# Two PEER blocks on one core: row pieces of the modulation on VectorE, other fillers, eight places for the value tiles

## The reference, cut to what matters

```python
mod = einsum('bd,de->be', c, w_mod) + b_mod
sh1, sc1, gt1, sh2, sc2, gt2 = split(mod, 6)
...
def peer_ffn(h, w_query, sub_keys, expert_u, expert_v):
    q = (h @ w_query)                          # 8 heads, two halves
    sc = einsum('bshpc,hpnc->bshpn', q, sub_keys)
    s1, i1 = top_k(sc[..., 0, :], 16); s2, i2 = top_k(sc[..., 1, :], 16)
    top_s, sel = top_k(s1[..., :, None] + s2[..., None, :], 16)   # over the 256 pairs
    idx = 128 * i1[sel] + i2[sel]; gates = softmax(top_s)
    a = gelu(einsum('cd,chkd->chk', x, expert_u[idx])) * gates
    return einsum('chk,chkd->cd', a, expert_v[idx])
```

## Time and profile before

| | us |
|---|---|
| median of 3 runs (lowest to highest) | 1972.68 (1967.51 to 1976.87) |
| the profiled execution | 1963.73 |
| its span | 1961.9 |
| PE, DVE, ACT, POOL busy | 1893.8, 1622.2, 1085.0, 568.2 |

### The profile page before, as it was taken

How to read it: one execution, slowest core, us unless ns; L and a number is a source line. 1 busy time by engine, 2 the same in 40 slices (tenths; PEclk the granted TensorE clock), 3 DMA queues, 4 the chain that set the end, 5 groups by cost and what they waited for, 6 DMA issues and landing times.

```text
span 1961.9 us, 36055 instructions
## 1 busy us (share of the span) xinstructions
PE 1893.8 (97%) x13546; PEld 1841.5 (94%) x13546; DVE 1622.2 (83%) x3384; ACT 1085.0 (55%) x2128; POOL 568.2 (29%) x498
## 2 busy tenths in 40 slices
PE   7999889999999999999999999999999999999997
PEld 5998889999999999999999988999999999999997
DVE  3777768889899989889777775588888998898997
ACT  3345555644566665555556554465445665555554
POOL 0000221444533234445200000034354332444351
PEclk8999999999999999999999999999999999999999
DMA  8764667678699899999856672566887898999995
GB/s 345 271 236 162 254 210 228 226 271 310 242 319 317 303 358 360 347 347 356 321 204 203 252 252 79 169 213 218 285 290 267 316 319 298 343 356 345 361 337 194
DMA packets 143469, 543.85 MB, mean 277 GB/s; under 512 B 15744, under 2 KB 16128, under 8 KB 138432
## 3 DMA queue, kind: packets, MB, share of 16 engines
q1 hardware_dynamic: 99312, 363.38, 52.7%
q0 software_dynamic: 40608, 160.06, 22.5%
q10 hardware_dynamic: 3376, 18.11, 2.5%
HBM read 539.78 MB, written 1.05 MB: 276 GB/s over the span
## 4 chain that ended last, share of the span: by engine, by line
PE 66%; DVE 13%; DMA 9%; issue 6%; ACT 5%; POOL 1%; SPq 0%; ACTq 0%; DVEq 0%; POOLq 0%
PE PB L1021 16%; PE PB L997 14%; PE PB L1022 7%; DVE WL L1813 5%; DMA RING<-in_v 5%; PE PB L994 4%; PE PB L959 4%; PE PB L586 4%; PE PB L587 4%; PE PB L588 4%; DMA RING<-in_u 3%; ACT WH L1324 2%; PE PB L992 2%; PE PB L908 2%; DVE AR L1838 1%
## 5 line engine op out<-in xcount | busy, mean ns | idle before, releaser
L1813 DVE TENSOR_TENSOR WL<-RING,WH 128x1024 fp32r<-128x1024 f32 x517 | 640.0, 1240 | 194.1 <-ACT WH L1324 190.1
L1324 ACT ACTIVATE WH<-RING 128x1024 fp32r<-128x1024 f32 x517 | 545.4, 1056 | 446.2 <-DMA RING<-in_v 161.2
L1021 PE MATMUL PB<-HX,WH 128*128 128x384 f32 x2048 | 587.7, 360 | 8.0 <-DVE WL L1813 7.4
L1022 PE MATMUL PB<-HX,WL 128*128 128x192 f32 x2048 | 512.7, 250 | 0.0
L1021 PEld LDWEIGHTS PB<-HX,WH 128*128 128x128 f32 x2048 | 384.5, 188 | 12.3 <-issue 11.7
L1022 PEld LDWEIGHTS PB<-HX,WL 128*128 128x128 f32 x2048 | 391.1, 191 | 0.0
L997 PE MATMUL PB<-AR,RING 128*128 128x192 f32 x2144 | 372.1, 326 | 0.0
L997 PEld LDWEIGHTS PB<-AR,RING 128*128 128x128 f32 x2144 | 348.1, 190 | 0.0
L2571 POOL DMA_INDIRECT AR<-in_v,SPX x128 | 244.6, 1911 | 320.8 <-DVE AR L2284 268.1
L994 PE MATMUL PB<-HX,WH 128*128 128x384 f32 x854 | 254.1, 361 | 0.0
L992 PE MATMUL PB<-HX,WL 128*128 128x192 f32 x976 | 227.8, 254 | 0.0
(11 more groups left out here) (277 smaller groups left out, 2891.2 us busy)
## 6 DMA issues: line engine op xcount, KB each, us to landing
RING<-in_u SPq DMA_DIRECT2D x256, 512.0 KB
RING<-in_v SPq DMA_DIRECT2D x256, 512.0 KB
RING<-in_win SPq DMA_DIRECT2D x90, 512.0 KB
AR<-in_wr POOLq DMA_DIRECT2D x24, 1024.0 KB, 5.4
RING<-in_wq SPq DMA_DIRECT2D x32, 512.0 KB
AR<-in_wr ACTq DMA_DIRECT2D x12, 1024.0 KB, 6.6
AR<-in_wm SPq DMA_DIRECT2D x8, 1024.0 KB, 16.4
RING<-in_wout SPq DMA_DIRECT2D x16, 512.0 KB
```

The lines of the kernel that those rows point to most:

```text
L1021: e.matmul(both_parts(c), hi(n_v + n)[:, cs], dense(k), start=start, stop=False)
L1022: return e.matmul(PB[c][:, 0:T], lo(n_v + n)[:, cs], HH[:, k, 0:T], start=False, stop=stop)
L1324: e.activation(hi(t), raw(("w", t), words(t)), ACT.Copy).then_inc(s_hi, 1)
L1813: e.tensor_tensor(lo(t), raw(("w", t), words(t)), hi(t).bitcast(F32), ALU.subtract).then_inc(s_lo, 1)
```

## The change

1. **Row pieces.** POOL's products and ACT's sums are gone. Chunks 24 to 27 are summed by DVE in the queries, where chunks 28 to 31 were; these go to up tiles 1, 4, ... 22 of block 1, one half each (`ROW_AT`). The four places of these chunks are given out anew (`NEXT_SLOT`), and POOL issues the eight loads as places come free.
2. **Silu** moves on ACT from before the output projection to after the second split of the query tiles; one table load fewer stands ahead of the projection.
3. **`choice_turns`** counts 130 for each row piece that is still to come. The table holds for both blocks, though only block 1 has row pieces. Done selection steps before and after the change are 30 and 22 at tile 16, 52 and 48 at tile 36, 65 and 59 at tile 45, 93 and 90 at tile 62, and 114 at tile 81 in both. `PK` comes at tile 45 where it came at tile 41; `DOT_AT` stays. `PAIRED` goes from tiles 17-20 and 58-61 to 24-26 and 61-63, `EQUALS` from 28-41 and 69-82 to 33-45 and 70-82, and POOL has 39 of the adds of a block where it had 34.
4. **Fillers.** New: 10 before the third chunk at the start, 4 and 4 in the first input projection, 3 ahead of the query tiles of block 1, 3 and 3 while block 2's norm waits. Those before the transposes of block 1's second norm go from 12 to 16.
5. **`norm_mod` on ACT** alternates `turned` and `high`.
6. **Value tiles** use eight places: the four of `RING` and four of `MORE` (a region that the up stage uses for the selection). `SLOT_PLAN` names the place of each load. The first loads into `MORE` wait until the up tiles are used up (`s_used` at `W_V`); before, the load of tile `W_V + 4` waited for tile `W_V` alone.

```diff
+ROW_AT = {1 + 3 * i: (28 + i // 2, i % 2) for i in range(8)}
...
-        share, count = sum(work) * min(j + 1, JG - 2) / (JG - 2), 0
+        rows = 130 * sum(i <= j for i in ROW_AT)
+        share, count = (sum(work) + 130 * len(ROW_AT)) * min(j + 1, JG - 2) / (JG - 2) - rows, 0
...
+def slot_plan():
+
+    last, used, plan = [-1] * (NSLOT + N_MORE), [0] * (NSLOT + N_MORE), []
+    for f, (kind, i) in enumerate(PLAN):
+        deep = kind == "w" and any(v + NSLOT <= i < v + NK for v in (W_V, W2_V))
+        s = min(range(NSLOT + N_MORE if deep else NSLOT), key=lambda n: last[n])
+        used[s] += 1
+        plan.append((s, last[s], used[s]))
+        last[s] = f
+    return plan
...
+        MORE = ar(28672, N_MORE, SLOTW)
...
-                if f >= NSLOT:
-                    was, n = PLAN[f - NSLOT]
+                s, prior, _ = SLOT_PLAN[f]
+                if s >= NSLOT and i in range(W_V, W_V + 2 * NSLOT):
+                    e.wait_ge(s_used, W_V)
+                if s >= NSLOT and i in range(W2_V, W2_V + 2 * NSLOT):
+                    e.wait_ge(s_used, W2_V)
+                if prior >= 0:
+                    was, n = PLAN[prior]
...
+                        if (c, a) == (0, 0) and kk in (2, 4):
+                            busy(2 if kk == 2 else 3, 4)
...
             transposed(0)
+            busy(3, 10)
             mod_chunk(2)
...
-            for n in (7, 8):
-                e.wait_ge(s_xu, n)
-                busy(6, 2)
+            e.wait_ge(s_xu, 7)
+            busy(6, 3)
+            e.wait_ge(s_xu, 8)
+            busy(6, 4)
             e.wait_ge(s_sq, 9)
-            busy(6, 1)
+            busy(6, 2)
...
             for g in range(20, 24):
                 columns(g)
+            busy(3, 3)
...
+            for n in (14, 15):
+                e.wait_ge(s_bt, n)
+                busy(1, 3)
             e.wait_ge(s_bt, 16)
...
-                turned(0)
-                turned(1)
-                high(0)
-                turned(2)
-                high(1)
-                turned(3)
-                high(2)
-                high(3)
+                for kp in range(4):
+                    turned(kp)
+                    high(kp)
...
-            e.wait_ge(s_crx, 16)
-            e.activation(CRX, CRX, ACT.Silu).then_inc(s_silu, 1)
             sqrt_table()
-            def product_sum(g):
...
-                if i in (5, 6):
-                    product_sum(19 + i)
...
             fill(W_WQ + 1)
+            e.wait_ge(s_crx, 16)
+            e.activation(CRX, CRX, ACT.Silu).then_inc(s_silu, 1)
...
                             if blk == 0 and t in (7, 9, 11, 13):
-                                row_sum(28 + (t - 7) // 2, 0)
-                                row_sum(28 + (t - 7) // 2, 1)
+                                row_sum(24 + (t - 7) // 2, 0)
+                                row_sum(24 + (t - 7) // 2, 1)
...
+                    if blk == 0 and j in ROW_AT:
+                        row_sum(*ROW_AT[j])
                     for _ in range(choose_steps(j)):
                         next(steps, None)
```

More of the change, by code:

```diff
@@ L76 @@
 ROW_LAND = {g: sum(ROW_SLOT[h] == s for h in ROW_SLOT if h <= g) for g, s in ROW_SLOT.items()}
-N_EARLY = 8
-N_MID = 8
-N_PROD = 4
-NEXT_SLOT = {24: 1, 25: 2, 26: 1, 27: 2, 28: 0, 29: 3, 30: 1, 31: 2}
-NEXT_LAND = {g: sum(NEXT_SLOT[h] == NEXT_SLOT[g] for h in NEXT_SLOT if h <= g) for g in NEXT_SLOT}
-def summed_before(g):
-    return g - 24 - N_PROD
 OUT_ORDER = [(0, 0), (1, 0), (0, 1), (1, 1), (2, 0), (2, 1), (3, 0), (3, 1)]
@@ L293, in two_block_kernel @@
         s_fg = [sem("s_fg1"), sem("s_fg2")]
-        s_slot = [sem(f"s_slot{i}") for i in range(NSLOT)]
+        s_slot = [sem(f"s_slot{i}") for i in range(NSLOT + N_MORE)]
         s_hi, s_lo, s_used = sem("s_hi"), sem("s_lo"), sem("s_used")
@@ L454, in raw @@
         def raw(what, n=SLOTW):
-            return RING[:, PLACE[what] % NSLOT, 0:n]
+            s = SLOT_PLAN[PLACE[what]][0]
+            return RING[:, s, 0:n] if s < NSLOT else MORE[:, s - NSLOT, 0:n]
         def landed(e, what):
-            f = PLACE[what]
-            e.wait_ge(s_slot[f % NSLOT], 16 * (f // NSLOT + 1))
+            s, _, count = SLOT_PLAN[PLACE[what]]
+            e.wait_ge(s_slot[s], 16 * count)
         def hi(n):
@@ L1529, in out_proj @@
                         square(X[:, a, 256 * c:256 * c + 256], a, c, 256).then_inc(s_sq, 1)
-            e.wait_ge(s_crx, 16)
-            e.activation(CRX, CRX, ACT.Silu).then_inc(s_silu, 1)
             sqrt_table()
-            def product_sum(g):
-                e.wait_ge(s_prod, g - 23)
-                for j in range(2):
-                    w, c = row_chunk(g)[:, j, :], 2 * g + j
-                    r = e.activation(w, w, ACT.Copy, accum_out=MC[:, c:c + 1])
-                r.then_inc(s_msum, 1)
             for i, (c, u) in enumerate(OUT_ORDER):
                 fill(W_OUT + i + 1, NW if i < 7 else 2)
-                if i in (5, 6):
-                    product_sum(19 + i)
                 if u:
@@ L1574, in peer @@
                             copy(qP[:, t, :], PB[1 + t % 3][:, 256:512], s_qc)
-                            if blk == 0 and t in (6, 8):
-                                product_sum(23 + t // 2)
                 step = 0
@@ L2628, in load @@
                 e.dma_start(row_chunk(g), row_source(g)).then_inc(chunk_landed(g)[0], 16)
-            def products(g):
-                e.wait_ge(*chunk_landed(g))
-                for j in range(2):
-                    w = row_chunk(g)[:, j, :]
-                    r = e.tensor_tensor(w, w, CRX, ALU.mult)
-                r.then_inc(s_prod, 1)
             load(24)
             load(25)
-            e.wait_ge(s_silu, 1)
-            products(24)
-            products(25)
-            for g in (26, 27):
-                e.wait_ge(s_msum, g - 25)
-                load(g)
-            products(26)
-            products(27)
             e.wait_ge(s_mcol, nth(24))
-            load(28)
-            load(29)
-            for g in (30, 31):
-                e.wait_ge(s_msum, g - 27)
+            load(26)
+            load(27)
+            for g, done in ((29, 1), (30, 2), (28, 3), (31, 4)):
+                e.wait_ge(s_mdv, done)
                 load(g)
```

25 lines of the change are left out of this document (14 added, 11 removed).

## The result

The changed kernel took 1977.03 us (median of 22 runs, 1971.34 to 1992.65), the kernel before on the same chips 1970.70. The ratio is **1.0043, with a 95% interval of 1.0025 to 1.0060**: some 8 us slower. The forecast was 1970.6 us, 2 us faster than before. The measured time lies in its range of 1956 to 1987, but on the other side of no change. The profiled execution of the changed kernel has a span of 1973.6 us, 11.7 more than before, and it is this difference that is taken apart here. So 5.3 of the 11.7 us come from which executions were profiled, and no run shows in which rows of the table they lie.

The account below looks back on a forecast made before the run. PE was taken as the bound, with 66% of the chain that ended last. The terms summed to -2.1 us on the profiled 1963.7, giving 1961.6; with 8.95 to the median the forecast was 1970.6 us, range 1956 to 1987.

Parts of the forecast that it names:

- Part 3: Up tiles 0 to 45 of block 1: DVE's slack takes the row pieces, +0.7 us for late single tiles, bounds 0 and +3.
- Part 1: Output projection of block 1 with silu and POOL's products gone: -12 us, bounds -9 and -13.5.
- part 2: Queries of block 1: two pairs of ACT sums leave the stage, -0.5 us, between -1 and +0.5.
- Parts 4 and 5: Up tiles 46 to 83, both blocks: late first gather, +10.8 us, and crowded DVE behind it, +8 us.
- The five effects: Output projection of block 1: waits, low clock and a slow norm step go, -1.9, -1.7, -2.0, -3.8 and -4.0, together -13.4 us.
- the fillers' price: Output projection of block 1: three fillers ahead of the queries +0.9 us; four before the transposes 1.2, filling an existing wait.
- Part 4: First gathers before tile 50: the later index write makes PE stand still, +5.3 us in block 1, +5.5 in block 2.
- The rival that rested on it: First gathers: the gather lands before DVE comes to it, costing 0; total 1959.8 us, chance 0.05.
- Part 5: Up tiles 50 to 83, both blocks: more selection steps, lowered clock and late steps, +4 us per block, +8.
- The slow rival: Selection bounds DVE up to tile 83, old slack unusable: 14 us per block, 28; total 1985 us, chance 0.20.
- Part 6: Value tiles: eight places remove late loads, -8 us for both stages, bounds -11 and -3.
- Part 7: Fillers at the start 0 us, bounds -5 and +3; in block 2's norm -1.1 us, bounds -1.7 and +0.4.

Follow-up runs that it names:

- n4: e1 with the fillers and norm_mod of the kernel before; ratio to before 0.9936.
- n1: e1 with the eight row pieces of chunks 28 to 31 cut to 16 of 1024 columns, loads kept; ratio to before 0.9921.
- n2: e1 with the loads of chunks 28 to 31 cut to 16 of 1024 columns, the pieces' work kept; ratio to before 0.9930.
- e2: The kernel before with only the new choice_turns, no row pieces in the up tiles; ratio to before 1.0117.
- e4: The changed kernel with the first twelve gathered products four tiles later; median 1967.59 us, ratio to before 0.9989.
- e1: The changed kernel with choice_turns as before in both blocks, all else kept; median 1961.94 us, ratio to before 0.9964.
- e3: The kernel before with only the eight places of the value tiles; ratio to before 0.9942.

## Why the prediction was wrong, point by point

Three terms of the sum failed, and with them its sign. Part 3 took it that DVE's slack of 13.6 us hides the row pieces, and gave their loads no time: +0.7 forecast, +5.0 measured. Part 1 priced the fillers as if the wait they stand in stayed, and left out the loads of the projection's tiles: -12.5 with part 2, -9.2 measured. Parts 4 and 5 put DVE's wait for POOL at tile 43 at nothing: +18.8 forecast, +24.3 measured, 3.2 of it this wait. The late gather itself was foreseen as it came.

That the time lies in the range is in part luck. Between the profiled executions the sum was -2.1 us and +11.7 were measured, 13.8 apart. The forecast added 8.95 us to come from the profiled execution to the median; for the changed kernel they lie 1.7 apart, and so only 6.4 of the 13.8 us are left in the median.

**Part 1, the output projection** (forecast -12, with part 2 -12.5; measured -9.2). The five effects came as forecast: no table load, the norm's step (L1869, now L1878) at 0.17 us, clock 1.00, the four waits of the earlier trace rows gone. The failing term is the fillers' price, put at +0.9. "The four more before the transposes fill a wait that PE has anyway": that wait was POOL's doing and went with the products, so the fillers ended on the path: 1.9 us, of which 1.0 would be there with the old ones too (n4), and 0.9 more directly ahead of the queries. n4, without the new ones, has the stretch 1.7 us shorter, at the cost of the clock. A further 1.39 us is a new wait at 231.9 us: PE got through the projection faster than its tiles were loaded (ACT waited 4.9 us for a load there). And the sum was loose: -13.4 with fillers at 0.9 and 1.2 us is -11.3, not -11.6, and -12 was taken.

**Part 3, up tiles 0 to 42 of block 1** (+0.7, bounds 0 and +3; measured +5.0). This is the largest miss of one part. "Net 3.5 more fit in": DVE's slack of 13.6 us was taken as a sum over 110 us. But in tiles 0 to 44 of the change DVE is idle for 14.0 of 116.6 us and PE for 5.5 all the same (second of the windows above): room in one tile does not give back what PE has waited in another. (Of the five additions counted here, POOL takes over only three before tile 45; part 5 has the other two.) And a piece is dearer here than in the queries: 1.22 us was its price there, and in the up tiles it lies beside POOL's additions. DVE's first piece and POOL's additions at that place:

```profile
308.38 1.62 DVE L1847 CUSTOM_DVE_ANT_0 AR<-AR 128x1024 f32<-128x1024 f32 x1
```

```profile
307.66 2.79 POOL L2591 TENSOR_TENSOR AR<-AR 128x192 f32<-128x192 f32 x2 [9.49 <-ACT AR L1622]
311.98 0.59 POOL L2591 TENSOR_TENSOR AR<-AR 128x192 f32<-128x192 f32 x1 [1.53 <-ACT AR L1622]
```

The piece takes 1.62 us, and POOL's two additions 2.79 where one alone takes 0.59 (second row). Over the sixteen pieces of chunks 24 to 31 the mean is 1.36 us, 1.22 for those of before. The Trainium skill, page "SBUF — State Buffer", section "Who interferes with whom", says it: a VectorE instruction with two SBUF inputs contends with a GpSimd instruction that reads SBUF. These rows agree: both take longer side by side. For the sum it is small, 8 times 0.3 us. n1 puts the pieces' work at 4.8 us in these tiles with the old turns, n2 the loads at 2.3; the load's share was not in the sum at all. The loads of moved pieces were moved too, and that was not followed. In the change itself 3.6 of the 5.0 us lie in tiles 0 to 15, right behind ACT's wait of 7.0 us for a load. How they divide between work and loads under the new turns, no run shows.

**Part 4, the first gather** (+10.8; the distance from the end of tile 44 to the start of tile 50 went from 13.06 to 18.76 us in block 1 and from 12.92 to 19.40 in block 2, +12.2). The mechanism was right, and its terms nearly so: 18.4 was forecast. The gather was usable 11.75 and 12.39 us after the write, forecast 11.5 (the 0.7 us for the notice in it has no row of its own). What was mis-sized is when the write comes, 1.6 us after the end of tile 44 and not 0.95. e2 and e4 show the cause: the table alone makes it, and four tiles' distance removes it.

The page "DMA: Bandwidth & Descriptors" of the Trainium skill, section "Anatomy of one DMA — SWDGE (gpsimd) path", gives a POOL-issued DMA 2.0 us and its bytes at 436 GB/s; worked out from that (an estimate), this chain takes near 7 us. The rows above do not agree: the two copies alone took 4.97 us from their issue at 421.05 to the issue of the gather at 426.02, and the first gather 6.2 us from there. The rival that rested on it fell.

**Part 5, up tiles 50 to 82** (+8; the span from tile 50 to 83 is longer by 4.6 and 4.3 us, +8.9). Right in size and kind. Beside it stands a wait that was not foreseen: DVE for POOL's products at tile 43, 1.6 us per block. It is in e2 and e4 too, and not in e1. `EQUALS` had been read in the diff and not followed to who waits at its end. With the part 4 excess this makes 24.3 where parts 4 and 5 had 18.8. The slow rival (28) was nearer in size than the forecast, though its mechanism, slack that can't be used up to tile 83, holds only for part of it by e4.

**Part 6, the value tiles** (-8; measured -9.1, and e3 alone 0.9942). Right. Not counted was that the last two up tiles take 0.7 to 0.8 us longer per block in the change; over the kernels this varies from nothing to 3.5 us.

**Part 7** (0 and -1.1; measured -0.3 and +0.2). The start came out even only because the profiled execution of before was itself slow there; over the kernels the fillers cost 2.3 us. e3 has the code of before up to there and is 2.2 us earlier without any edit. So the 0 came out by luck.

Together: +3.3 for the fillers and the load in part 1, +4.3 in part 3, +5.5 in parts 4 and 5, +1.8 at the end of the up stages and +1.0 elsewhere, -1.1 in part 6, and -1.0 in block 2's first tiles: the 13.8 us between -2.1 and +11.7.

## What to carry to other kernels

A step that is moved takes its producers, its consumers and its loads with it: where a table of turns is recomputed for one block's extra work, look at every fixed place that reads the table's results (here `DOT_AT`), in the other block too. Slack summed over a stage does not hide a wait in one tile of it; price an addition against the room between two neighbouring deadlines. And a filler is free only while the wait it stands in is there: if the same change removes that wait, remove the filler.
